# Broadcasting the mean and rstd of a layer norm through a DRAM scratch, in an eight-core encoder block on Trainium2

## The chip, the cores and the metric

The kernel runs on all 8 cores of one Trainium2 chip, with the same program on each core and no exchange between cores. The metric is the device time in microseconds (us) of the slowest core. Inside a core the engines are PE (TensorE, matrix products), DVE (VectorE), ACT (ScalarE), POOL (GpSimd) and SP (SyncE, which here only issues DMAs). Each engine runs its own list of instructions in order and waits on semaphores.

## The reference

One encoder block works on `x` of 4 sequences, 4096 tokens, 1024 channels. What matters here is the convolution branch and what is merged with it:

```
a = a_val * sigmoid(a_gate)                     # two products with w_in
a = depthwise_conv(a, w_dw, width 31) + b_dw
mu   = mean over the 1024 channels of a         # per token
rstd = rsqrt(mean((a - mu)^2) + 1e-5)           # per token
y_conv = silu((a - mu) * rstd * ln_g + ln_b) @ w_conv_out
merged = gateA * y_conv + gateB * y_pool        # y_pool: pooling branch
h = h + merged @ w_o
h = h + swiglu(rms_norm(h));  out = rms_norm(h)
```

The mean and the rstd are one number per token, and each is applied to all 1024 channels of that token.

## The kernel before, in words

Each core has 2048 tokens and works on them in two tiles of 1024 tokens; a tile has two blocks `b` of 512 tokens. Channels lie on partitions (8 groups `c` of 128) and tokens in the free dimension. A tile goes through these stages:

1. P1 (`P1_STEPS`): products with `w_in`, convolution and pooling. `conv(c)` (line 511) leaves the convolution output in `d_sb[:, c, b, :]`, and DVE adds it and its square up over `c` into `acc_s[:, b, :]` and `acc_q[:, b, :]` (128 x 512, f32).
2. P2 (`P2_STEPS`, a list written by hand): G steps (`gates`, line 656, four groups of 8 matmuls of 512 columns, each evicted by a Tanh on ACT), P steps (`pool_out`, line 673, two groups, evicted by DVE into `sgB`) and Y steps (`conv_out`, line 685, one group for one block `b`, which reads `actT[:, 0..7, b, :]`, evicted by two DVE instructions). The order is G0 G1 P0 P1 G2 P2 G3 Y0.0 Y1.0 Y2.0 Y0.1 Y1.1 Y2.1, and then the rest.
3. The product with `w_o`, the SwiGLU with its two large products (`ffn`, `down`), and the stores.

The layer norm is laid into P2 by the table `ln_plan` (line 646), whose keys are (G step, group in it). After the first two groups of G0, `ln_sums(b)` (line 598) sums `acc_s` and `acc_q` over the partitions with 8 matmuls against a column of ones, each with one output column, so that the sums of token 128*j + p stand on partition p, column j. Four small DVE instructions and one power on POOL (line 611) make mean and rstd of the block: 4 columns each in `lnst`, on 128 partitions.

To be applied, the two must stand on every partition, with the 512 tokens in the free dimension. Before, this takes two functions for each block `b` and each of mean and rstd (`w` = 0 and 1). `ln_spread(b, w)` (line 613) writes `tn` = identity times the column, 128 x 512 in f32, on DVE (line 619). `ln_bcast(b, w)` (line 621) multiplies it in f32 with the 128 x 128 matrix of ones on PE, which puts the values on all partitions of a PSUM bank, and ACT copies the bank into `acc_s` or `acc_q` (line 626), whose sums are no longer needed. The trace shows each such f32 product as two matmul records. The `order` rows show it as one row.

`ln_chunk(c, b)` (line 631) then applies mean and rstd to one channel group of one block: two DVE instructions (lines 637, 638) and a Silu on ACT (line 639) into `actT`. There are 16 chunks in a tile. They stand in the queue `lnq`, and `ln_step` takes one of them after each group of 8 matmuls in the G, P and Y steps.

PSUM has 8 banks that `nb()` gives out in turn, one to a group of matmuls, so PE can be at most 8 groups ahead of the evictions. Weights come in units of 256 KB by DMAs that POOL issues (`prefetch`, line 352) into a ring of 21 buffers. SP issues the other loads: in the first tile, ahead of P2, `invc` and two loads of `gb` (lines 888 to 890), and after step Y2.1 three loads of `xt` (`xres_load`, line 697), which lie over `acc_s`, `acc_q` and `sq` in memory. `xbar_transpose` (line 427) issues DMA transposes from SP in later stages.

Of the kernel before, what the change touches and what calls it, by code (L numbers as in the profile page):

```python
# [12 lines left out]
KC = 8  # L13
# [202 lines left out]
def build_nc():  # L216
    nc = bass.Bass("TRN2", target_bir_lowering=False)
    S = Sched(nc)
# [97 lines left out]
    def nb():  # L316
        b = bank[0]
        bank[0] = (b + 1) % 8
        return b

    def sem(name):
        return nc.alloc_semaphore(name)
# [5 lines left out]
    SP = Rec("sp", sem("s_sp"))  # L328
    gb_sem = [Prod(sem(f"d_gb{i}"), 16) for i in range(3)]
    tr_sem = [Prod(sem(f"d_tr{i}"), 16) for i in range(17)]  # L330
    wpt_sem = [Prod(sem(f"d_wpt{i}"), 16) for i in range(2)]
    cst = [Prod(sem(f"d_cst{i}"), 16) for i in range(3)]
    ring_sem = [Prod(sem(f"d_wr{i}"), 16) for i in range(RING)]
# [264 lines left out]
    def ln_sums(b):  # L598
        bk = nb()
        for w, acc in ((0, acc_s), (1, acc_q)):  # L600
            for j in range(4):
                o = psum[bk][:, w * 4 + j:w * 4 + j + 1]
                mm(o, acc[:, b, j * 128:j * 128 + 128], ones[:, 0:1], True, True, w == 1 and j == 3)
        mean4, msq4, rstd4 = (lnst[:, b * 16 + 4 * k:b * 16 + 4 * k + 4] for k in range(3))
        ps4, pq4 = psum[bk][:, 0:4], psum[bk][:, 4:8]
        S.op(DVE, lambda e: e.tensor_scalar(out=mean4, in0=ps4, scalar1=1.0 / D, scalar2=None, op0=ALU.mult), [ps4], [mean4])
        S.op(DVE, lambda e: e.tensor_tensor(out=msq4, in0=mean4, in1=mean4, op=ALU.mult), [mean4], [msq4])
        S.op(DVE, lambda e: e.scalar_tensor_tensor(out=msq4, in0=pq4, scalar=1.0 / D, in1=msq4, op0=ALU.mult, op1=ALU.subtract),
             [pq4, msq4], [msq4])
        S.op(DVE, lambda e: e.tensor_scalar(out=msq4, in0=msq4, scalar1=LN_EPS, scalar2=None, op0=ALU.add), [msq4], [msq4])  # L610
        S.op(POOL, lambda e: e.tensor_tensor(out=rstd4, in0=msq4, in1=nhalf[:, 0:4], op=ALU.pow), [msq4, nhalf[:]], [rstd4])

    def ln_spread(b, w):
        src = lnst[:, b * 16 + 8 * w:b * 16 + 8 * w + 4]
        dg = tn[w * 2 + b][:]
        o3 = dg.rearrange("p (j t) -> p j t", j=4)
        i0 = ident[:].unsqueeze(1).to_broadcast([128, 4, 128])
        i1 = src.unsqueeze(2).to_broadcast([128, 4, 128])
        S.op(DVE, lambda e: e.tensor_tensor(out=o3, in0=i0, in1=i1, op=ALU.mult), [ident[:], src], [dg])

    def ln_bcast(b, w):
        bm = nb()
        dg = tn[w * 2 + b][:]
        mm(psum[bm][:], ones[:], dg, True, True, True)
        dst, pmi = (acc_s, acc_q)[w][:, b, :], psum[bm][:]
        S.op(ACT, lambda e: e.activation(out=dst, in_=pmi, func=AF.Copy), [pmi], [dst])

    ti = [0]
    lnq = []
# [11 lines left out]
    def ln_step():  # L641
# [2 lines left out]
            ln_chunk(c, b)  # L644

    ln_plan = {
        (0, 0): (lambda: ln_sums(0),),
        (0, 1): (lambda: ln_sums(1),),
        (0, 2): (lambda: ln_spread(0, 0), lambda: ln_spread(0, 1)),
        (0, 3): (lambda: ln_bcast(0, 0), lambda: ln_spread(1, 0), lambda: ln_spread(1, 1)),  # L650
        (1, 0): (lambda: ln_bcast(0, 1), lambda: lnq.extend((k, 0) for k in range(KC))),
        (1, 1): (lambda: ln_bcast(1, 0),),
        (1, 2): (lambda: ln_bcast(1, 1), lambda: lnq.extend((k, 1) for k in range(KC))),
    }

    def gates(c):
# [411 lines left out]
```

How the kernel before makes its waits and increments, by code:

```python
def replay(e, rec):  # L205
    for o in rec.ops:
        if o[0] == "wait":
            e.wait_ge(o[1], o[2])
        elif o[0] == "ins":
            r = o[1](e)
            if o[2]:
                r.then_inc(rec.sem, 1)
        else:
            e.dma_start(out=o[1], in_=o[2]).then_inc(o[3], 16)
# [212 lines left out]
    def xbar_transpose(rec, dsem, out_ap, in_ap):  # L427
        rg, wg = S._sets([in_ap], [out_ap], (), ())
        S._waits(rec, S._deps(rg, wg, dsem, dsem.count + 16))
        dsem.count += 16
        rec.ops.append(("ins", lambda e: e.dma_start_transpose(out_ap, in_ap).then_inc(dsem.sem, 16), False))
```

## Time and profile before

| what | value |
|---|---|
| three timed runs | 1027.54, 1030.3 and 1162.77 us; median 1030.3 |
| the profiled execution, its own time | 1026.95 us |
| its span on the slowest core (core 7) | 1025.4 us |
| spans of the eight cores | 1020.5 to 1025.4 us |
| granted TensorE clock, mean over the span, core 7 | 0.991 |
| PE busy, of the span | 98% |
| DVE / ACT / POOL busy, of the span | 42% / 27% / 17% |

The profiled execution is one run of the program. Its span goes from the first to the last instruction of core 7. Its own time is 1.55 us longer (1026.95 - 1025.4), which lies around the span. "Busy" of an engine counts its work and not its waits. The first tile's P2 begins at 155.3 us, the second tile's at 641.6 us.

### The profile page before, as it was taken

The page shows a single profiled execution, that of the slowest core. Times are in us where ns is not written, and L with a number is a line of the kernel's source. Part 1 is how long each engine was busy: PE and PEld are TensorE (multiplying, and loading weights), DVE is VectorE, ACT ScalarE, POOL GpSimd, SP SyncE. Part 2 cuts the span into 40 slices and gives each one's busy share as a digit, 9 for nine tenths or more (in the row PEclk, how much of TensorE's full clock was granted, in tenths as well). Part 3 has the DMA queues.
Part 4 walks back from the last instruction along what each step waited for, and adds up shares of the span by engine and source line. Part 5 has one row for each costly group of instructions (what it writes and reads, how often), then busy time and mean ns, then how long its engine had stood idle before and what let it go on. Part 6 is the DMA issues. An engine that isn't in the chain of part 4 may idle for free.

```text
span 1025.4 us, 16277 instructions; the slowest of 8 cores (1020.5 to 1025.4 us)
## 1 busy us (share of the span) xinstructions
PE 1001.4 (98%) x5606; PEld 475.1 (46%) x5606; DVE 431.4 (42%) x654; ACT 281.7 (27%) x490; POOL 178.3 (17%) x328
## 2 busy tenths in 40 slices
PE   6899999999999999999999999999999999999996
PEld 3556555444444444444444444544444444444442
DVE  5466555742472323211345566574247212111133
ACT  4234455512132222211113334451213211111111
POOL 3211422011122211110231111101113111111010
PEclk8999999999999999999999999999999999999999
DMA  8698997343389877640939988334336954554022
GB/s 223 98 203 180 182 246 131 86 81 62 64 190 175 162 112 126 94 66 1 175 104 250 205 147 163 59 92 73 62 67 152 152 75 73 78 81 65 1 72 102
DMA packets 80481, 121.29 MB, mean 118 GB/s; under 512 B 30833, under 2 KB 30833, under 8 KB 80402
## 3 DMA queue, kind: packets, MB, share of 16 engines
q0 software_dynamic: 38592, 70.27, 43.3%
q1 hardware_dynamic: 39506, 41.86, 16.4%
q10 hardware_dynamic: 2304, 8.13, 2.0%
q8 instruction: 47, 0.77, 0.3%
q14 instruction: 32, 0.26, 0.1%
HBM read 159.59 MB, written 8.39 MB: 164 GB/s over the span
## 4 chain that ended last, share of the span: by engine, by line
PE 96%; DMA 2%; DVE 1%; ACT 1%; issue 0%; SPq 0%; DVEq 0%; POOLq 0%; ACTq 0%
PE ps L382 90%; PE ps L522 6%; DMA h<-xe 2%; PE ps L414 0%; ACT sqj L392 0%; DVE ub L404 0%; SPq L214 0%; DVEq L949 0%; DVE s L559 0%; ACT sqj L750 0%; DVE h L748 0%; DVE uT L423 0%; POOLq L949 0%; ACT psb L545 0%; ACT sg L486 0%
## 5 line engine op out<-in xcount | busy, mean ns | idle before, releaser
L382 PE MATMUL ps<-vT,wr 128*128 128x512 bf16 x1408 | 304.9, 379 | 0.0
L382 PE MATMUL ps<-uT,wr 128*128 128x512 bf16 (+1 forms) x1472 | 290.5, 356 | 2.1 <-ACT sqj L392 2.1
L214 POOL DMA_DIRECT2D wr<-wst x268 | 142.9, 535 | 688.9 <-PE ps L382 631.2
L382 PEld LDWEIGHTS ps<-vT,wr 128*128 128x128 bf16 x1408 | 137.6, 98 | 165.2
L382 PEld LDWEIGHTS ps<-uT,wr 128*128 128x128 bf16 x1472 | 143.8, 99 | 143.8 <-issue 12.3
L730 DVE TENSOR_TENSOR fT<-ps,sgf 128x512 bf16<-128x512 f32 x88 | 60.9, 692 | 217.5 <-PE ps L382 195.4
L382 PE MATMUL ps<-wr,fT 128*128 128x512 bf16 x704 | 152.3, 379 | 0.0
L729 ACT ACTIVATE sgf<-ps 128x512 f32<-128x512 f32 x88 | 52.5, 597 | 229.0 <-PE ps L382 229.0
L382 PEld LDWEIGHTS ps<-wr,fT 128*128 128x128 bf16 x704 | 68.9, 98 | 83.1
L522 PE MATMUL ps<-rep,wr 128*32 128x512 bf16 x1024 | 59.9, 388 | 2.1 <-DVE s L559 2.1
L748 DVE TENSOR_TENSOR h<-ps,h 128x512 f32<-128x512 f32 x32 | 22.1, 692 | 84.3 <-PE ps L382 84.3
L382 PE MATMUL ps<-m2T,wpf 128*128 128x512 bf16 x256 | 57.5, 379 | 0.0
L382 PE MATMUL ps<-actT,wr 128*128 128x512 bf16 x256 | 57.2, 379 | 0.0
L750 ACT ACTIVATE sqj<-h 128x512 bf16<-128x512 f32 x32 | 20.1, 630 | 134.0 <-DVE h L748 134.0
L382 PE MATMUL ps<-wr,mergedT 128*128 128x512 bf16 x256 | 55.6, 379 | 0.0
L679 DVE SCALAR_TENSOR_TENSOR sgB<-sgB,ps 128x512 f32<-128x512 f32 x32 | 21.9, 686 | 72.7 <-PE ps L382 72.5
L665 ACT ACTIVATE sgA<-ps,pc_s 128x512 f32<-128x512 f32 x32 | 21.8, 681 | 102.5 <-PE ps L382 101.5
L392 ACT ACTIVATE sqj<-h 128x1024 bf16<-128x1024 f32 x24 | 25.4, 1057 | 64.1 <-DVE h L708 53.4
L522 PEld LDWEIGHTS ps<-rep,wr 128*32 128x32 bf16 x1024 | 26.7, 98 | 33.1 <-issue 9.7
L486 ACT ACTIVATE sg<-ps 128x352 f32<-128x352 f32 (+1 forms) x40 | 20.7, 517 | 69.4 <-PE ps L382 57.8
L382 PEld LDWEIGHTS ps<-m2T,wpf 128*128 128x128 bf16 x256 | 25.0, 98 | 30.2
L382 PEld LDWEIGHTS ps<-wr,mergedT 128*128 128x128 bf16 x256 | 25.0, 98 | 30.2
(75 smaller groups left out, 616.0 us busy)
## 6 DMA issues: line engine op xcount, KB each, us to landing
wr<-wst POOLq DMA_DIRECT2D x268, 256.0 KB, 5.4
rep<-aT SPq DMA_DIRECT2D x256, 65.8 KB, 5.5
xt<-xe SPq DMA_DIRECT2D x24, 512.0 KB, 4.5
out<-h ACTq DMA_DIRECT2D x15, 512.0 KB, 2.8
h<-xe SPq DMA_DIRECT2D x8, 512.0 KB, 7.2
wpt<-wpt SPq DMA_DIRECT2D x4, 256.0 KB, 9.3
gb_s<-gb SPq DMA_DIRECT2D x2, 512.0 KB, 10.9
out<-h ACTq DMA_DIRECT2D x1, 256.0 KB, 2.1
```

Of the source, the lines that this page charges most:

```text
L214: e.dma_start(out=o[1], in_=o[2]).then_inc(o[3], 16)
L382: S.op(PE, lambda e: e.matmul(out, lhsT=lhsT, rhs=rhs, start=start, stop=stop), [lhsT, rhs], [out], signal=signal)
L392: S.op(ACT, lambda e: e.activation(out=sqj[0:n, :], in_=src, func=AF.Square, scale=1.0 / 32.0, accum_out=ms), [src], [sqj[0:n, :], ms])
L486: S.op(ACT, lambda e: e.activation(out=sgo, in_=pgi, func=AF.Tanh, scale=0.5), [pgi], [sgo])
L522: S.op(PE, lambda e, o=o, lt=lt, r_=r_, q=q, j=j: e.matmul(o, lhsT=lt, rhs=r_, start=(q == 0), stop=(q == 7), tile_position=(0, 32 * j)), ...
L665: S.op(ACT, lambda e, o=o, p_=p_, bia=bia: e.activation(out=o, in_=p_, func=AF.Tanh, bias=bia, scale=0.5), [p_, bia], [o])
L679: S.op(DVE, lambda e, t=t, p_=p_: e.scalar_tensor_tensor(out=t, in0=t, scalar=1.0, in1=p_, op0=ALU.add, op1=ALU.mult), [p_, t], [t])
L729: S.op(ACT, lambda e: e.activation(out=so, in_=pgi, func=AF.Silu), [pgi], [so])
L730: S.op(DVE, lambda e: e.tensor_tensor(out=fo, in0=pui, in1=so, op=ALU.mult), [pui, so], [fo])
L748: S.op(DVE, lambda e, ho=ho, pdi=pdi: e.tensor_tensor(out=ho, in0=pdi, in1=ho, op=ALU.add), [pdi, ho], [ho])
L750: S.op(ACT, lambda e, ho=ho, sh=sh: e.activation(out=sqj[:, 0:512], in_=ho, func=AF.Square, scale=1.0 / 32.0, accum_out=sh), [ho], [sqj[:, ...
```

## The change

`ln_spread` is gone, and `ln_bcast(b)` now does mean and rstd of a block by DMAs from SP: one DMA stores the 8 columns of `lnst` (128 partitions x 8 values of 4 bytes) into a DRAM scratch `lscr[b]`, in the order of the tokens, so that the values of neighbouring partitions stand 4 bytes apart and those of one partition 512 bytes apart. SP waits on the semaphore of this store (`ls_sem`). Then two DMAs read the 512 mean values and the 512 rstd values for every one of the 128 partitions and write them into `acc_s[:, b, :]` and `acc_q[:, b, :]` (256 KB each). Both count on one semaphore (`lb_sem[b]`), and a reader waits for both. In `lnst` the rstd takes the columns beside the mean.

In `ln_plan`, `ln_bcast(b)` follows `ln_sums(b)` in the first two groups of G0. The chunks of block 0 are queued one group later than before, at (1, 1); those of block 1 at (1, 2) as before.

```diff
--- before.py
+++ after.py
@@ -226,6 +226,8 @@
     ic_d = nc.dram_tensor("invc", [128, 32], F32, kind="ExternalInput")
     out_d = nc.dram_tensor("out", [TOK, D], F32, kind="ExternalOutput")
 
+    lscr = nc.dram_tensor("lscr", [2, 2, 512], F32, kind="Internal")
+
     base0 = (nc.sbuf_base + 63) // 64 * 64
     top = nc.sbuf_top
 
@@ -328,6 +330,8 @@
     SP = Rec("sp", sem("s_sp"))
     gb_sem = [Prod(sem(f"d_gb{i}"), 16) for i in range(3)]
     tr_sem = [Prod(sem(f"d_tr{i}"), 16) for i in range(17)]
+    ls_sem = [Prod(sem(f"d_ls{i}"), 16) for i in range(2)]
+    lb_sem = [Prod(sem(f"d_lb{i}"), 16) for i in range(2)]
     wpt_sem = [Prod(sem(f"d_wpt{i}"), 16) for i in range(2)]
     cst = [Prod(sem(f"d_cst{i}"), 16) for i in range(3)]
     ring_sem = [Prod(sem(f"d_wr{i}"), 16) for i in range(RING)]
@@ -601,7 +605,7 @@
             for j in range(4):
                 o = psum[bk][:, w * 4 + j:w * 4 + j + 1]
                 mm(o, acc[:, b, j * 128:j * 128 + 128], ones[:, 0:1], True, True, w == 1 and j == 3)
-        mean4, msq4, rstd4 = (lnst[:, b * 16 + 4 * k:b * 16 + 4 * k + 4] for k in range(3))
+        mean4, msq4, rstd4 = (lnst[:, b * 16 + 4 * k:b * 16 + 4 * k + 4] for k in (0, 2, 1))
         ps4, pq4 = psum[bk][:, 0:4], psum[bk][:, 4:8]
         S.op(DVE, lambda e: e.tensor_scalar(out=mean4, in0=ps4, scalar1=1.0 / D, scalar2=None, op0=ALU.mult), [ps4], [mean4])
         S.op(DVE, lambda e: e.tensor_tensor(out=msq4, in0=mean4, in1=mean4, op=ALU.mult), [mean4], [msq4])
@@ -610,20 +614,19 @@
         S.op(DVE, lambda e: e.tensor_scalar(out=msq4, in0=msq4, scalar1=LN_EPS, scalar2=None, op0=ALU.add), [msq4], [msq4])
         S.op(POOL, lambda e: e.tensor_tensor(out=rstd4, in0=msq4, in1=nhalf[:, 0:4], op=ALU.pow), [msq4, nhalf[:]], [rstd4])
 
-    def ln_spread(b, w):
-        src = lnst[:, b * 16 + 8 * w:b * 16 + 8 * w + 4]
-        dg = tn[w * 2 + b][:]
-        o3 = dg.rearrange("p (j t) -> p j t", j=4)
-        i0 = ident[:].unsqueeze(1).to_broadcast([128, 4, 128])
-        i1 = src.unsqueeze(2).to_broadcast([128, 4, 128])
-        S.op(DVE, lambda e: e.tensor_tensor(out=o3, in0=i0, in1=i1, op=ALU.mult), [ident[:], src], [dg])
-
-    def ln_bcast(b, w):
-        bm = nb()
-        dg = tn[w * 2 + b][:]
-        mm(psum[bm][:], ones[:], dg, True, True, True)
-        dst, pmi = (acc_s, acc_q)[w][:, b, :], psum[bm][:]
-        S.op(ACT, lambda e: e.activation(out=dst, in_=pmi, func=AF.Copy), [pmi], [dst])
+    def ln_bcast(b):
+        S.wait_prod(SP, lb_sem[b])
+        o_ = lscr.ap()[b].rearrange("w (j p) -> p (w j)", p=128)
+        i_ = lnst[:, b * 16:b * 16 + 8]
+        rg, wg = S._sets([i_], [], (), ())
+        S._waits(SP, S._deps(rg, wg, ls_sem[b], ls_sem[b].count + 16))
+        ls_sem[b].count += 16
+        SP.ops.append(("ins", lambda e: e.dma_start(out=o_, in_=i_, allow_slow_non_contiguous=True).then_inc(ls_sem[b].sem, 16), False))
+        S.wait_prod(SP, ls_sem[b])
+        tot = lb_sem[b].count + 32
+        for w in range(2):
+            src = bass.AP(tensor=lscr, offset=(b * 2 + w) * 512, ap=[[0, 128], [1, 512]])
+            S.dma(SP, lb_sem[b], (acc_s, acc_q)[w][:, b, :], src, val=tot)
 
     ti = [0]
     lnq = []
@@ -644,13 +647,10 @@
             ln_chunk(c, b)
 
     ln_plan = {
-        (0, 0): (lambda: ln_sums(0),),
-        (0, 1): (lambda: ln_sums(1),),
-        (0, 2): (lambda: ln_spread(0, 0), lambda: ln_spread(0, 1)),
-        (0, 3): (lambda: ln_bcast(0, 0), lambda: ln_spread(1, 0), lambda: ln_spread(1, 1)),
-        (1, 0): (lambda: ln_bcast(0, 1), lambda: lnq.extend((k, 0) for k in range(KC))),
-        (1, 1): (lambda: ln_bcast(1, 0),),
-        (1, 2): (lambda: ln_bcast(1, 1), lambda: lnq.extend((k, 1) for k in range(KC))),
+        (0, 0): (lambda: ln_sums(0), lambda: ln_bcast(0)),
+        (0, 1): (lambda: ln_sums(1), lambda: ln_bcast(1)),
+        (1, 1): (lambda: lnq.extend((k, 0) for k in range(KC)),),
+        (1, 2): (lambda: lnq.extend((k, 1) for k in range(KC)),),
     }
 
     def gates(c):
```

PE, first tile, from the sums of block 1 to the first P step (`wr` are the ring's weights, `tn` the identity products, `m2T` the input of the P steps); before:

```order
L382 MATMUL ps<-ones_s,acc_q 128x1 x4
L382 MATMUL ps<-uT,wr_62 128x512 x8
L382 MATMUL ps<-uT,wr_63 128x512 x8
L382 MATMUL ps<-tn_139,ones_s 128x512
L382 MATMUL ps<-uT,wr_43 128x512 x8
L382 MATMUL ps<-tn_141,ones_s 128x512
L382 MATMUL ps<-uT,wr_44 128x512 x8
L382 MATMUL ps<-tn_140,ones_s 128x512
L382 MATMUL ps<-uT,wr_43 128x512 x8
L382 MATMUL ps<-tn_142,ones_s 128x512
L382 MATMUL ps<-uT,wr_44 128x512 x8
L382 MATMUL ps<-m2T,wpf 128x512 x32
```

and now:

```order
L386 MATMUL ps<-ones_s,acc_q 128x1 x4
L386 MATMUL ps<-uT,wr_62 128x512 x8
L386 MATMUL ps<-uT,wr_63 128x512 x8
L386 MATMUL ps<-uT,wr_43 128x512 x8
L386 MATMUL ps<-uT,wr_44 128x512 x8
L386 MATMUL ps<-uT,wr_43 128x512 x8
L386 MATMUL ps<-uT,wr_44 128x512 x8
L386 MATMUL ps<-m2T,wpf 128x512 x32
```

The four products of `tn` with `ones_s` between the groups of 8 are gone from PE; nothing else on it has another place.

SP, first tile, from the last convolution input to the first `xt` load, with the waits; before:

```order
L214 DMA invc_s<-invc 128x32
L214 DMA gb_s<-gb 128x1024 x2
L214 DMA xt_90<-xe 128x1024 [waits s_act,s_dve]
L214 DMA xt_91<-xe 128x1024 [waits s_act,s_dve]
L214 DMA xt_92<-xe 128x1024
```

and now:

```order
L214 DMA invc_s<-invc 128x32
L214 DMA gb_s<-gb 128x1024 x2
L624 DMA lscr<-lnst 128x8x1 [waits s_pool]
L214 DMA acc_s<-lscr 128x512 [waits d_ls0,s_dve,s_pe]
L214 DMA acc_q<-lscr 128x512 [waits s_dve]
L624 DMA lscr<-lnst 128x8x1 [waits s_pool]
L214 DMA acc_s<-lscr 128x512 [waits d_ls1,s_dve,s_pe]
L214 DMA acc_q<-lscr 128x512 [waits s_dve]
L214 DMA xt_90<-xe 128x1024 [waits d_lb0,s_dve,d_lb1]
L214 DMA xt_91<-xe 128x1024 [waits s_dve]
```

Six DMAs stand between the `gb` loads and the `xt` loads. The store of block 0 waits for POOL's power. The first broadcast waits for that store, and the store of block 1 stands behind both broadcasts of block 0.

DVE, first tile, from the second of the four identity products (`tn` from `ident_s`) to the first eviction of a P step (`sgB`); L637 and L638 are a chunk; before:

```order
L619 TENSOR_TENSOR tn_141<-ident_s,lnst 128x512
L619 TENSOR_TENSOR tn_140<-ident_s,lnst 128x512
L619 TENSOR_TENSOR tn_142<-ident_s,lnst 128x512
L637 TENSOR_TENSOR tn_139<-d_sb,acc_s 128x512
L638 TENSOR_TENSOR tn_139<-tn_139,acc_q 128x512
L637 TENSOR_TENSOR tn_140<-d_sb,acc_s 128x512
L638 TENSOR_TENSOR tn_140<-tn_140,acc_q 128x512
L637 TENSOR_TENSOR tn_141<-d_sb,acc_s 128x512
L638 TENSOR_TENSOR tn_141<-tn_141,acc_q 128x512
L637 TENSOR_TENSOR tn_142<-d_sb,acc_s 128x512
L638 TENSOR_TENSOR tn_142<-tn_142,acc_q 128x512
L679 SCALAR_TENSOR_TENSOR sgB_131<-sgB_131,ps 128x512
```

and now, from the last small instruction of the sums of block 1 (L640 and L641 are a chunk):

```order
L614 TENSOR_SCALAR lnst<-lnst 128x4
L640 TENSOR_TENSOR tn_139<-d_sb,acc_s 128x512
L641 TENSOR_TENSOR tn_139<-tn_139,acc_q 128x512
L640 TENSOR_TENSOR tn_140<-d_sb,acc_s 128x512
L641 TENSOR_TENSOR tn_140<-tn_140,acc_q 128x512
L640 TENSOR_TENSOR tn_141<-d_sb,acc_s 128x512
L641 TENSOR_TENSOR tn_141<-tn_141,acc_q 128x512
L679 SCALAR_TENSOR_TENSOR sgB_131<-sgB_131,ps 128x512
```

The identity products (three of the first tile's four stand above) are gone, and three chunks instead of four stand ahead of the first `sgB` eviction, because the chunks are queued one group later. 

## Rows read from the trace of the kernel before

**Rows 1.** The page: busy time, TensorE clock by slice, chain that ended last

```profile
PE 1001.4 (98%) x5606; PEld 475.1 (46%) x5606; DVE 431.4 (42%) x654; ACT 281.7 (27%) x490; POOL 178.3 (17%) x328
...
PEclk8999999999999999999999999999999999999999
...
PE 96%; DMA 2%; DVE 1%; ACT 1%; issue 0%; SPq 0%; DVEq 0%; POOLq 0%; ACTq 0%
```

**Rows 2.** Groups of instructions by line, whole span

```profile
L382 PE MATMUL ps<-tn,ones_s 128*128 128x512 f32 x16 | 8.2, 592 | 0.0
...
L619 DVE TENSOR_TENSOR tn<-ident_s,lnst 128x512 f32<-128x512 bf16 x8 | 5.2, 688 | 0.7 <-POOL lnst L611 0.7
```

**Rows 3.** PE in order of time, first tile: start us, us, instruction

```profile
155.32 1.91 PE L382 MATMUL ps<-uT,wr 128*128 128x512 bf16 x8
...
165.67 1.02 PE L382 MATMUL ps<-tn,ones_s 128*128 128x512 f32 x2
166.53 1.90 PE L382 MATMUL ps<-uT,wr 128*128 128x512 bf16 x8
168.26 1.02 PE L382 MATMUL ps<-tn,ones_s 128*128 128x512 f32 x2
...
200.26 4.05 PE L382 MATMUL ps<-actT,wr 128*128 128x512 bf16 x18
```

**Rows 4.** All engines in order of time, first tile, POOL's power and first chunk

```profile
160.14 1.04 POOL L611 TENSOR_TENSOR lnst<-lnst,nhalf_s 128x4 f32<-128x4 f32 x1 [3.65 <-DVE lnst L610]
...
167.62 0.69 DVE L637 TENSOR_TENSOR tn<-d_sb,acc_s 128x512 f32<-128x512 f32 x1 [1.05 <-ACT acc_s L626]
```

**Rows 5.** The same view, DVE and ACT in the middle of the chunks

```profile
184.03 0.68 DVE L679 SCALAR_TENSOR_TENSOR sgB<-sgB,ps 128x512 f32<-128x512 f32 x1
...
184.63 0.68 DVE L637 TENSOR_TENSOR tn<-d_sb,acc_s 128x512 f32<-128x512 f32 x1
...
186.02 0.69 DVE L637 TENSOR_TENSOR tn<-d_sb,acc_s 128x512 f32<-128x512 f32 x1
...
198.97 0.81 ACT L639 ACTIVATE actT<-tn,pc_s 128x512 bf16<-128x512 f32 x1
```

**Rows 6.** POOL's power and PE in the second tile, in order of time

```profile
641.59 1.91 PE L382 MATMUL ps<-uT,wr 128*128 128x512 bf16 x8
...
646.40 1.04 POOL L611 TENSOR_TENSOR lnst<-lnst,nhalf_s 128x4 f32<-128x4 f32 x1 [3.67 <-DVE lnst L610]
```

**Rows 7.** Line 431, the DMA transposes: issue to landing

```profile
DMA to landing us min/median/max: 3.1/3.7/8.7
```

**Rows 8.** DMA queues, 325 to 336 us, one transpose and one xt load

```profile
q1 hardware_dynamic: 1199, 0.79, 46.4%
...
uT<-ub SPq DMA_TRANSPOSE x1, 8.7
```

**Rows 9.** SP's DMA issues in order of time, first tile, before P2

```profile
142.19 0.90 SPq L214 DMA_DIRECT2D gb_s<-gb  x2
```

**Rows 10.** The page: DMA queues and issues, us to landing at the end

```profile
q0 software_dynamic: 38592, 70.27, 43.3%
...
xt<-xe SPq DMA_DIRECT2D x24, 512.0 KB, 4.5
...
gb_s<-gb SPq DMA_DIRECT2D x2, 512.0 KB, 10.9
out<-h ACTq DMA_DIRECT2D x1, 256.0 KB, 2.1
```

**Rows 11.** Five-microsecond stretches: PEclk, DMA share and GB/s stand last

```profile
160.00:165.00 5.00, 5.00 (x33) 3.26 (x31) 1.95 (x6) 1.37 (x2) 2.28 (x2) 1.00 1.09 187
165.00:170.00 5.00, 5.00 (x21) 2.25 (x20) 1.98 (x3) 2.57 (x4) 1.26 (x3) 1.00 0.96 161
170.00:175.00 5.00, 5.00 (x21) 2.27 (x20) 3.50 (x6) 3.31 (x6) 0.53 (x1) 1.00 0.06 10
645.00:650.00 5.00, 5.00 (x34) 3.31 (x34) 1.63 (x9) 0.69 (x1) 1.21 (x2) 1.00 0.01 2
```

## The prediction

> **What bounds the kernel now.** I read the page first. PE is busy for 98% of the span, the chain that ended last runs over PE for 96% of it, and the granted clock is 0.9 or more in all slices but the first [rows 1]. In the stretches that matter here it is 1.00, the 2.4 GHz level [rows 11]. So whatever leaves PE's list shortens the kernel by its own length, as long as nobody makes PE wait afterwards. Next I looked for what the change removes. The list of groups has 16 matmul records of `ps<-tn,ones_s`, two for each f32 product: 8 products, four to a tile [rows 2]. Their price is not the 8.2 us of that row, because neighbouring matmuls overlap. It has to be read from PE in order of time: such a product begins at 165.67 and the next group of 8 at 166.53, so it takes 0.86 us of PE's time. The group of 8 takes 168.26 - 166.53 = 1.73 us [rows 3]. Last I looked for the slack behind the mean and rstd, on DVE and ACT, since the change makes them come later.
>
> **The change part by part.**
>
> *Removed from PE:* 8 products by 0.86 us = 6.9 us, all on the path. *Removed from DVE:* 8 identity products of 0.69 us, and from ACT as many copies; both engines are busy for 42% and 27% of the span [rows 1, 2], and at this place they stand ahead of the chunks, so I count them at nothing in themselves. They did set when the chunks began.
>
> *Added on SP's queue:* per block one store and two broadcasts. SP is idle there: behind the six DMAs of a tile wait only the three `xt` loads, which need the last chunk anyway. Issuing two such loads took SP 0.90 us [rows 9], and nobody waits for that.
>
> *Added wait:* the first chunk on DVE now waits until mean and rstd of block 0 have landed. Call this time T, and S the time from the store's issue to its landing. The store can go when POOL's power ends, 160.14 + 1.04 = 161.2 us [rows 4], so at about 161.3. Then the two broadcasts (512 KB together) follow, with a landing time like a 512 KB load, 4.5 us, against 10.9 us for the two `gb` loads beside full queues [rows 10]; with SP's wake-up I take 5. T = 161.3 + S + 5. Before, the first chunk began at 167.6 [rows 4].
>
> *How late may T be?* Behind the waiting chunk on DVE stand all 16 chunks and the `sgB` evictions of the P steps; behind the Silu on ACT stand the Tanh evictions of the G steps. PE goes on until it needs a bank or a chunk's result. A chunk takes DVE 186.02 - 184.63 = 1.39 us, an eviction between two chunks 0.60 (184.03 to 184.63), the Silu 0.81 [rows 5]. Six evictions (P0, P1, P2) fall among the 16 chunks: 16 x 1.39 + 6 x 0.60 = 25.8, with the Silu and a handover of 0.1 the last `actT` is there at T + 26.8. The reader is Y0.1. Y0.0 began at 200.26 [rows 3]; without four products of 0.86 it begins at 196.8, Y0.1 three groups later at 202.0, and its eighth matmul, which reads the last channel group, 7/8 of a group later at 203.5. So T may be as late as 203.5 - 26.8 = 176.7. The eight banks give a looser bound: by the same walk over ACT's list, T up to some 179.
>
> *S* is not in this trace: no transfer has 4-byte pieces. The store has 128 x 8 = 1024 of them, since neither side joins two values (the values of a partition lie 512 bytes apart in DRAM); over 16 engines that is 64 each. The nearest thing in number is a DMA transpose: in 325 to 336 us the queue q1 moved 1199 packets and 0.79 MB; one `xt` load of 0.52 MB is 128 of them, so a transpose is about 1070 packets of 256 bytes. They cost 0.464 x 16 x 11 / 1199 = 68 ns each, and the transpose landed after 8.7 us, beside weight loads [rows 8]; the median of all transposes is 3.7 and the least 3.1 [rows 7]. The dear end is the mean packet of the weight queue q0, 0.433 x 16 x 1025.4 / 38592 = 184 ns [rows 10]. In the first tile the DMA engines are full from 160 to 170 us (share 1.09 and 0.96) and idle from 170 to 175 (0.06); in the second they are idle at the store (0.01) [rows 11]. So S is bounded from below by 3.1. From above, 64 packets of 184 ns plus 2.1 us, the shortest landing of a store to DRAM [rows 10], give 13.9 with idle queues; with the queues full each packet also waits for one of q0, if they take turns: 64 x (184 + 68) ns + 2.1 = 18.2. I take the transposes, which agree in number of packets and differ in size: S = 8.7 in the first tile, 3.7 in the second.
>
> *First tile:* T = 161.3 + 8.7 + 5 = 175.0, which is 1.7 before the limit: no stall. The second block's store goes at about 171 and its broadcasts land at about 171 + 3.7 + 5 + 2 = 182, while DVE asks for them after 8 chunks and 4 evictions, at T + 13.5 = 188.5. *Second tile:* P2 begins at 641.59 against 155.32 [rows 3, 6], so the limit is 176.7 + 486.3 = 663.0; the power ends at 647.4 [rows 6], T = 647.6 + 3.7 + 5 = 656.3. No stall, 6.7 us to spare.
>
> By the Trainium skill ("DMA: Bandwidth & Descriptors", Rules for kernel authors) a pattern whose last dimension is not contiguous becomes one descriptor per element; that would be the same 1024, and no run here shows it yet.
>
> *Sum, against the profiled execution's own time:* 1026.95 - 6.9 + 0 = 1020.05. The values 1026.95, 1027.54 and the median 1030.3 of before have a mean of 1028.3, 1.3 above the profiled one, so I forecast 1020.05 + 1.35 = 1021.4 us.
>
> **The rivals.** *A, the late store, slower than before.* If 4-byte writes to DRAM cost much more than 256-byte packets to SBUF, T passes the limit and PE waits for it microsecond by microsecond. First tile: T - 176.7 = S - 10.4; for its second block, T2 = 161.3 + S + 0.9 (two issues) + S + 5 against T + 13.5, so S - 12.6 more; the second tile gives about the same. With one S for all, 4S - 46 us. That eats the gain of 6.9 at S = 13.2, which is the point from which the kernel is slower than before; it costs 2% beyond that (27.5 us in all) at S = 18.4. At my upper bounds (S = 18.2, then 13.9) the stalls are 7.8 + 5.6 + 3.5 + 1.3 = 18.2, and the time is 1021.4 + 18.2 = 1039.6. For it: the slack in the first tile is only 1.7 us by my sum, the queues are full there, neighbouring values of 4 bytes are written by different descriptors, and DVE has no room to catch up (1.39 + 0.60 in a P group against 1.73 of PE). Against it: 68 ns a packet gives 4.4 us of work, and the DMA engines fall idle at 170 us. The Trainium skill ("DMA: Bandwidth & Descriptors", Specifications) says that pieces under 512 bytes make the DMA engine read, modify and write. If that doubles a packet of 68 ns, S grows by 4.4 to 13.1 in the first tile and 8.1 in the second, and the stalls are 2.7 + 0.5 = 3.2: the time would be 1024.6. The 256-byte packets of the transposes are under that size too and landed in 3.7 us, but in SBUF, so the trace neither confirms nor denies it.
>
> *B, part of the gain lost.* S between 10.4 and 13.2 in the first tile, or broadcasts near the 10.9 us of the `gb` loads: T at 177 to 182, a stall of 1 to 5 us, once or twice. Time about 1025.
>
> *C, the freed time is handed back elsewhere.* The broadcasts write 2 MB more into SBUF beside the weight loads, and PE takes the weights 3.5 us sooner in each P2. If the weights were near their limit, PE would meet that as a new wait on `wr`, and the time would stay at about 1028. Against it: the idle DMA stretch from 170 us on, and no `PE <- DMA` anywhere on a 96% PE chain.
>
> **How the numbers follow.** Forecast 0.55, A 0.20, B 0.13, C 0.07; the remaining 0.05 is what I haven't seen, in either direction. The likeliest gives 1021.4. Its own range is 1017 to 1025: 3 to 4 us for the spread of the runs. Up to 1034 the range takes in B, C and the milder part of A (S to about 15), so that about 2 in 10 is left out, nearly all above. A difference of 2% is about what a measurement of this kernel tells from no change. Nothing here can give 20 us, so faster by over 2% gets 0.03. Slower by over 2% needs S over 18 or a second effect: 0.10, half of A. The rest, 0.87, is within 2%.
>
> **What would show it.** Right: no `tn,ones_s` records; the groups of 8 in G1 start 1.73 us apart; the first chunk starts between 172 and 177 us; Y0.0 at about 196.8; PE has no idle time between 155 and 260. For S, the landing time of `lscr<-lnst`: 3 to 10 us. A is right if that is over 13 us and PE waits for `actT` or for a bank at Y0.1 and before. B shows as one such wait of a few us in the first tile only. C shows as PE waiting for `wr`. The prediction is wrong as to its mechanism if PE waits in P2 while the chunks come in time, or if the kernel gains more than 9 us.

## The result and the profile after

The changed kernel takes 1070.2 us in the median of 4 runs (1067.14 to 1072.51), against 1027.54 for the kernel before (1025.57 to 1030.3, 3 runs); the ratio is 1.041, with an interval of 1.037 to 1.046. It is slower by 4%, where 1021.4 us were forecast and 1034 was the upper end of the range. Runs in which a whole die was disturbed are left out, which below leaves one run of e4 and of e11 and two of e10. The profile is of core 3, the slowest; the cores' spans go from 1058.2 to 1071.0 us.

The page, with the rows that answer to [rows 1], and the waits of PE (us in total, times, longest):

```profile
PE 1004.1 (94%) x5590; PEld 473.2 (44%) x5590; DVE 424.3 (40%) x646; ACT 277.7 (26%) x482; POOL 177.5 (17%) x328
...
PEclk9999999799999999999999999978999999999999
...
PE ps L386 76%; DMA lscr<-lnst 7%; PE ps L526 5%; SPq L214 2%; DMA acc_q<-lscr 2%; DMA h<-xe 2%; DMA rep<-aT 1%; DVE tn L640 1%; PE ps L418 0%; DVE sgB L679 0%; ACT sgA L665 0%; DVE ub L408 0%; ACT sqj L396 0%; DVE tn L641 0%; ACT actT L642 0%
```

```profile
PE ps L386 <- ACT sgA L665: 38.3, 4, 17.6
PE ps L386 <- ACT actT L642: 6.2, 6, 1.1
```

The products are gone, but PE's busy share has fallen from 98% to 94%. DMA holds 11% of the chain that ended last, most of it the store `lscr<-lnst`. PE waits 38.3 us for a Tanh eviction and 6.2 us for chunks. The clock has a 7 in two slices, one in each P2.

PE in order of time, the two P2, which answers to [rows 3]:

```profile
156.18 1.89 PE L386 MATMUL ps<-uT,wr 128*128 128x512 bf16 x8
...
159.61 10.56 PE L386 MATMUL ps<-uT,wr 128*128 128x512 bf16 x48
...
176.91 3.63 PE L386 MATMUL ps<-uT,wr 128*128 128x512 bf16 x16
197.39 6.03 PE L386 MATMUL ps<-uT,wr 128*128 128x512 bf16 x16 [16.85 <-ACT sgA L665]
203.26 3.62 PE L386 MATMUL ps<-m2T,wpf 128*128 128x512 bf16 x16
...
215.22 6.59 PE L386 MATMUL ps<-actT,wr 128*128 128x512 bf16 x29 [1.41 <-ACT sgA L665]
222.83 0.38 PE L386 MATMUL ps<-actT,wr 128*128 128x512 bf16 x1 [1.02 <-ACT actT L642]
224.23 0.38 PE L386 MATMUL ps<-actT,wr 128*128 128x512 bf16 x1 [1.02 <-ACT actT L642]
225.68 5.52 PE L386 MATMUL ps<-actT,wr 128*128 128x512 bf16 x17 [1.07 <-ACT actT L642]
231.04 1.24 PE L386 MATMUL ps<-m2T,wpf 128*128 128x512 bf16 x5
```

```profile
686.18 3.63 PE L386 MATMUL ps<-uT,wr 128*128 128x512 bf16 x16
707.37 5.34 PE L386 MATMUL ps<-uT,wr 128*128 128x512 bf16 x16 [17.55 <-ACT sgA L665]
```

The six groups of G0 and G1 now run without a gap (48 matmuls in 10.4 us, 1.73 us a group), so the 0.86 us of each product is really gone. Then PE stands still for 16.85 us in the first tile and 17.55 in the second, both times before the third group of G2, which needs the bank of a Tanh that stands on ACT behind the first chunk's Silu. In the stop the granted clock has fallen to 0.50, the 1.2 GHz level: the 16 matmuls from 197.39 take 5.87 us until 203.26, where 3.46 are usual, and the 17 from 225.68 take 5.36 instead of 3.7.

```profile
190.00:195.00 5.00, 0.00 (x0) 0.00 (x0) 0.69 (x1) 0.00 (x0) 0.00 (x0) 0.50 0.09 7
```

(Busy time by engine, then PEclk, DMA share and GB/s.) SP's issues in order of time show where the time goes (start us, us):

```profile
158.67 0.38 SPq L624 DMA_DIRECT2D lscr<-lnst  x1
186.70 0.33 SPq L214 DMA_DIRECT2D acc_s<-lscr  x1
...
187.59 0.38 SPq L624 DMA_DIRECT2D lscr<-lnst  x1
197.61 0.32 SPq L214 DMA_DIRECT2D acc_s<-lscr  x1
```

```profile
668.00 0.39 SPq L624 DMA_DIRECT2D lscr<-lnst  x1
677.74 0.33 SPq L214 DMA_DIRECT2D acc_s<-lscr  x1
...
678.81 4.79 SPq L624 DMA_DIRECT2D lscr<-lnst  x1
714.88 0.32 SPq L214 DMA_DIRECT2D acc_s<-lscr  x1
```

SP issues a broadcast when it has seen the store land, so the distance is S, SP's wake-up included: 28.0 and 10.0 us for the two blocks of the first tile, 9.7 and 36.1 in the second. Over the eight cores S is 14.4 to 29.1 and 10.0 to 21.3 in the first tile, 9.4 to 19.3 and 20.5 to 36.1 in the second. The prediction took 8.7 and 3.7. The broadcasts are late too (the view of DMA issues, us to landing; the row of its own is DVE's wait for them):

```profile
acc_s<-lscr SPq DMA_DIRECT2D x4, 256.0 KB, 9.7
acc_q<-lscr SPq DMA_DIRECT2D x4, 256.0 KB, 10.5
...
lscr<-lnst SPq DMA_DIRECT2D x4, 4.0 KB, 18.9
```

```profile
DVE tn L640 <- DMA acc_q<-lscr: 76.0, 4, 34.1
```

What happens between is seen in the DMA queues of 162 to 166 us, of 166 to 170 and of 170 to 174 (packets, MB, share of the 16 engines):

```profile
q0 software_dynamic: 220, 0.39, 65.7%
q1 hardware_dynamic: 990, 0.00, 19.5%
...
wr<-wst POOLq DMA_DIRECT2D x2, 256.0 KB, 19.9
```

```profile
DMA packets 7, 0.01 MB, mean 2 GB/s; under 512 B 3, under 2 KB 3, under 8 KB 7
...
q0 software_dynamic: 4, 0.01, 8.4%
```

```profile
q0 software_dynamic: 84, 0.17, 112.1%
```

Nearly all 1024 pieces pass through the DMA engines in the first four microseconds (990 packets, 19.5% of 16 engines, so 0.195 x 16 x 4 / 990 = 12.6 ns each; in the second tile 1040 packets at 11.7% from 668 to 672 us, 7.2 ns each). SP sees their landing at 186.7, 20 us after nearly all of them had passed. For 4 us almost nothing else moves, 7 packets. Then the weights move again, but slowly: the 84 packets from 170 to 174 us take 1.121 x 16 x 4 / 84 = 0.85 us each, and 17 packets at 42.7% from 174 to 178 take 1.6 us each, where the mean before was 184 ns. From 182 to 186 us it is 0.18 us again. The two weight units issued between 162 and 166 us take 19.9 us to land, against a median of 5.8 on the page. So the cost is not in the engines' work on small packets, and it holds up the other queue. That it lies behind the engines, where the writes are finished, is inferred: no record shows the memory.

The 36.1 us of the last store have a second part. It is issued at 678.81, behind the broadcasts of block 0, which took 18.9 and 26.0 us to land, and its pieces pass only after 696 us (1023 packets until 700, some 60 of them the broadcast's by their size, and 101 more until 706):

```profile
q1 hardware_dynamic: 1023, 0.13, 40.4%
```

From 706 to 712 us the core moves one packet in all, and the store has landed at 714.9.

The sum by these rows, slowest core after against slowest core before: waits at the chunks 38.3 + 6.2 = 44.5, lower clock after the stops some 2.4 + 1.7 + 1.7 + 1.7 = 7.5 (the last taken equal to its twin of the first tile), removed products -6.9, together 45 us, against spans of 1071.0 - 1025.4 = 45.6.

### The profile page after: what moved, and what is told of

It is laid out like the page before. It is cut to its first block, busy times and chain, and to the rows that moved or that the text cites. A ratio compares the mean times of both kernels' runs of the same rounds, so it can differ in the third digit from the quotient of the medians.

```text
span 1071.0 us, 16234 instructions; the slowest of 8 cores (1058.2 to 1071.0 us)
## 1 busy us (share of the span) xinstructions
PE 1004.1 (94%) x5590; PEld 473.2 (44%) x5590; DVE 424.3 (40%) x646; ACT 277.7 (26%) x482; POOL 177.5 (17%) x328
## 4 chain that ended last, share of the span: by engine, by line
PE 82%; DMA 11%; SPq 2%; DVE 2%; issue 1%; ACT 1%; DVEq 0%; POOL 0%; POOLq 0%; ACTq 0%
PE ps L386 76%; DMA lscr<-lnst 7%; PE ps L526 5%; SPq L214 2%; DMA acc_q<-lscr 2%; DMA h<-xe 2%; DMA rep<-aT 1%; DVE tn L640 1%; PE ps L418 0%; DVE sgB L679 0%; ACT sgA L665 0%; DVE ub L408 0%; ACT sqj L396 0%; DVE tn L641 0%; ACT actT L642 0%
## 5 line engine op out<-in xcount | busy, mean ns | idle before, releaser
L386 PE MATMUL ps<-actT,wr 128*128 128x512 bf16 x256 | 63.0, 400 | 10.1 <-ACT actT L642 6.2
L750 ACT ACTIVATE sqj<-h 128x512 bf16<-128x512 f32 x32 | 20.2, 631 | 133.7 <-DVE h L748 133.7
L640 DVE TENSOR_TENSOR tn<-d_sb,acc_s 128x512 f32<-128x512 f32 x32 | 21.9, 686 | 76.0 <-DMA acc_q<-lscr 76.0
L642 ACT ACTIVATE actT<-tn,pc_s 128x512 bf16<-128x512 f32 x32 | 26.1, 814 | 80.8 <-DVE tn L641 80.3
L386 PEld LDWEIGHTS ps<-actT,wr 128*128 128x128 bf16 x256 | 25.8, 102 | 45.6 <-issue 19.9
## 6 DMA issues: line engine op xcount, KB each, us to landing
gb_s<-gb SPq DMA_DIRECT2D x2, 512.0 KB, 10.4
```

Of the source, the lines that this page charges most:

```text
L386: S.op(PE, lambda e: e.matmul(out, lhsT=lhsT, rhs=rhs, start=start, stop=stop), [lhsT, rhs], [out], signal=signal)
L640: S.op(DVE, lambda e: e.tensor_tensor(out=t, in0=dso, in1=mean, op=ALU.subtract), [dso, mean], [t])
L642: S.op(ACT, lambda e: e.activation(out=ao, in_=t, func=AF.Silu, bias=lb, scale=lg), [t, lg, lb], [ao])
L750: S.op(ACT, lambda e, ho=ho, sh=sh: e.activation(out=sqj[:, 0:512], in_=ho, func=AF.Square, scale=1.0 / 32.0, accum_out=sh), [ho], [sqj[:, ...
```

## The experiments

The question was what makes the landing late. Eleven kernels were run, on three chips (e1 to e4, e5 to e8, e9 to e11), each against the kernel before on its own chip (medians 1028.1 to 1028.7 us). The edits are shortened to the lines that matter; e3 to e11 all have the line with `gb_d` that is shown with e3. Where the broadcasts read `gb` in place of the scratch (runs e3 to e11), mean and rstd are not applied, but every instruction has its size.

### Fewer pieces, and none

**e1.** Runs of 16 bytes: the sums are taken over every fourth token, so that a partition holds four neighbours.

```diff
-mm(o, acc[:, b, j * 128:j * 128 + 128], ones[:, 0:1], ...)
+mm(o, acc[:, b, :].rearrange("p (t j) -> p t j", j=4)[:, :, j], ones[:, 0:1], ...)
-o_ = lscr.ap()[b].rearrange("w (j p) -> p (w j)", p=128)
+o_ = lscr.ap()[b].rearrange("w (p j) -> p w j", j=4)
-i_ = lnst[:, b * 16:b * 16 + 8]
+i_ = lnst[:, b * 16:b * 16 + 8].rearrange("p (w j) -> p w j", j=4)
```

> The sums are taken over every fourth token, so that a partition holds four neighbouring tokens and the store is 256 runs of 16 bytes instead of 1024 of 4; all else is as in the changed kernel. Theory N (each small write to DRAM costs, one after another, at the memory): the wait for the store, 10 to 28 us in the changed kernel, falls to about a quarter plus a fixed part of 2 us, so 4 to 9 us, PE's waits at the chunks shrink from 44 us to under 5, and the time is about 1023 to 1030 us. Theory B (the bytes or the DRAM address are slow, not the number of pieces): the store still lands after 10 to 28 us and the time stays near 1070.

Measured: 1033.0 us, ratio 1.006 (1.004 to 1.008). S is 6.7 to 11.1 us in the first tile and 2.2 to 8.0 in the second, and PE has no wait for `sgA` or `actT` on the slowest core. So the store's wait fell as theory N has it. The time did not come down to the 1023 to 1030 expected, for reasons of the run's own. The first is weights of 128 columns that stand 16 bytes apart.

```profile
L386 PEld LDWEIGHTS ps<-ones_s,acc_s x32: 308/329/337, 155.3 to 654.3; 128*128 128x128 f32 x32
```

```profile
155.49 1.81 PE L386 MATMUL ps<-ones_s,acc_s 128*128 128x1 f32 x8
...
159.03 3.58 PE L386 MATMUL ps<-uT,wr 128*128 128x512 bf16 x8
162.40 1.82 PE L386 MATMUL ps<-ones_s,acc_s 128*128 128x1 f32 x8
```

A load takes 329 ns where it took 191 with neighbouring columns, and the sums of a block 3.54 us (155.49 to 159.03) where they took 1.72, four times in the kernel: 7.3 us. The second is the clock, which the sum of the experiment did not have: it fell during the first of these sums and was granted at 0.50 from 159 to 170 us of the first tile, while PE was busy without a gap, so that the group between the sums took 3.37 us (159.03 to 162.40) instead of 1.73; in the second tile the same group took 3.10 and the clock was back by 661 us. What set it off is not shown.

**e2.** Rows of 512 bytes: PE turns the eight columns round first.

```diff
+def ln_turn(b):
+    idf = tn[3][:, 0:128]                      # f32 identity, copied from ident in each tile
+    po, ro = psum[bk][0:8, 0:128], tn[2][0:8, b * 128:b * 128 + 128]
+    mm(po, lnst[:, b * 16:b * 16 + 8], idf, True, True, True)
+    S.op(DVE, lambda e: e.tensor_copy(out=ro, in_=po), [po], [ro])
-o_ = lscr.ap()[b].rearrange("w (j p) -> p (w j)", p=128);  i_ = lnst[:, b * 16:b * 16 + 8]
+o_ = lscr.ap()[b].rearrange("w (j p) -> (w j) p", p=128);  i_ = tn[2][0:8, b * 128:b * 128 + 128]
-    (0, 0): (ln_sums(0), ln_bcast(0)),  (0, 1): (ln_sums(1), ln_bcast(1)),
+    (0, 0): (ln_sums(0),),  (0, 1): (ln_sums(1),),
+    (0, 2): (ln_turn(0), ln_bcast(0)),  (0, 3): (ln_turn(1), ln_bcast(1)),
```

> Mean and rstd are turned on PE first (a product of the 8 columns with an f32 identity, copied from PSUM by DVE), and the store is 8 rows of 512 bytes. Adds 2 small f32 products and 3 small DVE copies to a tile. Theory N: the store lands after 2 to 3 us, PE does not wait in the chunks, and the kernel gains the 6.9 us of the removed products less some 0.3 us for each of 4 turns: 1022 to 1024 us, ratio to before 0.994 to 0.996. Theory R (a hot spot: 128 rows of each broadcast read the same 2 KB on every core at once): the broadcasts still land after 10 to 25 us, PE waits 10 us or more, and the time is above before's.

Measured: 1024.0 us in the median of 5 runs, ratio 0.9966 (0.9951 to 0.998): of the kernels that apply mean and rstd the only one that is faster than before, by 0.3%. PE in order of time:

```profile
165.21 0.38 PE L386 MATMUL ps<-tn,lnst 128*8 128x128 f32 x2
165.53 1.91 PE L386 MATMUL ps<-uT,wr 128*128 128x512 bf16 x8
...
198.85 10.52 PE L386 MATMUL ps<-actT,wr 128*128 128x512 bf16 x47
```

```profile
649.75 0.31 SPq L633 DMA_DIRECT2D lscr<-tn  x1
651.11 0.36 SPq L214 DMA_DIRECT2D acc_s<-lscr  x1
```

A turn costs PE 0.32 us (165.21 to 165.53). The first block's store of 8 rows lands after 1.4 us in the second tile (649.75 to 651.11) and 4.3 to 6.5 in the first; the second block's, behind the broadcasts, after 4.5 to 6.4 and 3.9 to 7.1. PE has no wait for a bank behind the chunks on any core, and none for a chunk but 2.0 us on core 7. The time is at the upper end of what was expected. Theory R is out: the broadcasts, 128 reads of one 2 KB row, land after 4.5 and 5.4 us (medians of the slowest core).

**e4.** No store; SP waits for POOL and issues the broadcasts, which read `gb`.

> No store at all; SP waits for POOL's power and then issues the two broadcasts of each block, which read the gains from another tensor, so mean and rstd are not applied. If the store is the whole cost (theories N, L, B): the broadcasts land after 4 to 6 us, PE does not wait in the chunks, and the time is the forecast 1021 to 1023 us. Theory R (reads of one 2 KB row by 128 partitions are slow): the broadcasts land after 10 us or more and PE waits for the chunks.

Measured: 1021.44 us, one run, 6.7 below the kernel before on that chip. The rest of the prediction, 6.9 us off the path and broadcasts that are early enough, gives the forecast number once the store is away.

### The spacing

**e3, e6, e11.** The same 1024 values of 4 bytes in one DMA, 256, 64 and 32 bytes apart. **e5.** The same, 4 bytes apart, as in the changed kernel.

```diff
-lscr = nc.dram_tensor("lscr", [2, 2, 512], F32, kind="Internal")
+lscr = nc.dram_tensor("lscr", [2, 2, 512, 64], F32, kind="Internal")    # 16 in e6, 8 in e11
-o_ = lscr.ap()[b].rearrange("w (j p) -> p (w j)", p=128)
+o_ = lscr.ap()[b].rearrange("w (j p) s -> p (w j) s", p=128)[:, :, 0:1]
-src = bass.AP(tensor=lscr, offset=(b * 2 + w) * 512, ap=[[0, 128], [1, 512]])
+src = bass.AP(tensor=gb_d, offset=w * 512, ap=[[0, 128], [1, 512]])     # alone in e5
```

> The same 1024 writes of 4 bytes, but each in its own 256 bytes of DRAM, so that no two share a line; the broadcasts read the gains from another tensor in place of the scratch, so mean and rstd are not applied. Theory N (number of partial writes): the store lands as late as in the changed kernel, 10 to 28 us, and the time is about 1060 to 1070. Theory L (neighbouring 4-byte values collide in one line or one bank and go one after another): the store lands after 3 to 6 us and the time is 1022 to 1030.

> The changed kernel's own dense store (1024 values of 4 bytes, neighbours 4 bytes apart), waited for as there, but the broadcasts read the gains from another tensor, so mean and rstd are not applied. It differs from the spread run in the spacing alone and from the changed kernel in the source of the broadcasts alone. Theory L (neighbouring values collide): the stores land after 10 to 36 us and the time is 1060 to 1070. Theory S (it was the source: reading lines that were just written is what is slow): the stores land within 10 us in the second tile and the time is near the spread run's 1028.

> As the spread run, with the 4-byte values 64 bytes apart instead of 256. Theory L with lines of 64 bytes or less: as the spread run, first store of the second tile in 3 to 4 us, time 1026 to 1030. If the unit in which they collide is larger (256 bytes or more), or it is the small area of DRAM that counts: the stores land between the two, 5 to 20 us in the second tile, and the time is 1035 or more.

> As the runs with spaced values, with the values 32 bytes apart (two to 64 bytes). If values collide within 32 bytes only: as at 64 and 256 bytes apart, 3 to 4 us for the first store of the second tile and 1026 to 1030 us. If the unit is 64 bytes: two writes to a line instead of sixteen, so somewhat slower, 4 to 8 us, and 1028 to 1038 us. Theory area: between dense and spaced, since the area is 32 KB instead of 64.

| run | bytes between values | time, us | ratio to before | S, second tile, first block | S, first tile, first block |
|---|---|---|---|---|---|
| e5 | 4 | 1080.4 | 1.052 (1.045 to 1.059) | 11.3 to 18.0 | 13.7 to 37.0 |
| e11 | 32 | 1032.9 (one run) | | 3.2 to 6.9 | 9.3 to 20.4 |
| e6 | 64 | 1028.0 | 0.9996 (0.998 to 1.001) | 3.0 to 4.4 | 13.1 to 20.5 |
| e3 | 256 | 1027.8 | 0.9997 (0.9986 to 1.0007) | 2.7 to 3.8 | 13.5 to 18.9 |

Each S is the spread over the eight cores, read from SP's issues as above. The slowest core of the dense run e5 and of e6:

```profile
680.86 0.39 SPq L624 DMA_DIRECT2D lscr<-lnst  x1
698.83 0.33 SPq L214 DMA_DIRECT2D acc_s<-gb  x1
```

```profile
652.99 0.39 SPq L624 DMA_DIRECT2D lscr<-lnst  x1
656.87 0.33 SPq L214 DMA_DIRECT2D acc_s<-gb  x1
```

The number of pieces, their size, the DMA and the wait are the same; only the distance differs, and 11.3 to 18.0 us become 3.0 to 4.4. That speaks against theory N, which wanted e3 as slow as the changed kernel, and against theory S. Theory L stands. Its time for e5, 1060 to 1070, was too low; why e5 is some 10 us above the changed kernel is open. e11 lies close to the spaced runs; from its single time nothing finer can be read than that most of the harm is gone at 32 bytes. What e3 and e6 still lack to e4's 1021.4 is the first tile: there S is 13 to 20 us in both, and PE waits 5.1 us (e3) and 7.6 us (e6) for `sgA`, on the slowest core. The queues of e6 from 170 to 174 us show why:

```profile
q0 software_dynamic: 289, 0.52, 100.3%
q1 hardware_dynamic: 292, 0.00, 7.6%
```

The pieces take turns with the weight packets one for one, and the weights fill the engines.

e1 belongs to this as well: its runs of 16 bytes stand four to 64 bytes, and they landed after 2.7 to 5.1 us (second tile, first block). So what is dear is 64 bytes that 16 single writes share; shared by four of 16 bytes, or by two of 4 bytes (e11), they were not.

**e9, e10.** A shared line, or a small area? 16 neighbours still share 64 bytes; in e9 each such line has its own 1024 bytes, in e10 the lines are dense. Both store by 8 DMAs of 16 partitions.

```diff
+for g in range(8):
+    o_ = lscr.ap()[b].rearrange("w (j g) s -> g s w j", g=8)[g, 0:16]    # lscr [2, 2, 32, 256] in e9, [2, 2, 32, 16] in e10
+    i_ = lnst[16 * g:16 * g + 16, b * 16:b * 16 + 8].rearrange("p (w j) -> p w j", j=4)
```

> Which is it, values that share 64 bytes, or a small area of DRAM? Here 16 neighbouring values still share 64 bytes, but each such line has its own 1024 bytes, so the area is 16 times as large as in the dense store (64 KB for a block, as in the run with values 64 bytes apart). The store is split into 8 DMAs of 16 partitions; SP waits for all of them; the broadcasts read the gains from another tensor, so mean and rstd are not applied. Theory line (values in one 64-byte line go one after another): stores land after 10 to 30 us, time 1050 to 1080. Theory area (a few banks take all the writes): as the runs with spaced values, 3 to 6 us in the second tile plus up to 3 us for the seven extra issues, time 1025 to 1035.

> The control of the run above: the same 8 DMAs of 16 partitions, with the lines one behind the other, which is the layout of the changed kernel. Under both theories the stores land after 10 to 30 us and the time is 1050 to 1085. If it is fast, splitting the DMA is itself a cure and the run above says nothing on the line.

Measured: e9 1086.0 us, ratio 1.056 (1.043 to 1.068); e10 1084.1 (mean of 1082.0 and 1086.2), ratio 1.054 (1.049 to 1.059). First stores land after 19.8 to 48.4 us in e9 and 31.1 to 40.9 in e10 (first tile), 10.4 to 26.8 and 12.9 to 24.7 (second). An area 16 times as large brings nothing if the lines stay shared; e6, with an area of the same size and no shared lines, is fast. So it is the values that share 64 bytes, and not the area. The split is no cure; that it does no harm of its own is read from e10 beside e5 (ratios 1.054 and 1.052), and a split store with 64 bytes for each value was not run. e9 is above the 1080 expected.

**e8.** The same 1024 pieces, written into SBUF.

```diff
-o_ = lscr.ap()[b].rearrange("w (j p) -> p (w j)", p=128)
+o_ = sq[b][:, 0:16].rearrange("p (c two) -> p c two", two=2)[:, :, 0:1]
```

> The same 1024 pieces of 4 bytes, waited for in the same way, but written into SBUF (every second element of 16 in each partition) instead of DRAM; the broadcasts read the gains from another tensor, so mean and rstd are not applied. If the price is of DRAM: the store lands after 3 to 4 us in the second tile and 5 to 18 us in the first (its 64 pieces an engine still take turns with weight packets), time 1021 to 1028. If 4-byte pieces are slow wherever they go: it lands after 10 us or more in the second tile too, time 1040 or more.

Measured: 1024.7 us, ratio 0.9968 (0.9954 to 0.9983). S is 2.5 to 5.0 us for the first block of the second tile, and 12.5 to 17.2 in the first tile. The first number is that of e6 (3.0 to 4.4): writes to DRAM that share nothing cost no more than writes to SBUF. That the collision is a matter of DRAM alone is not shown, since in SBUF no two partitions write into the same 64 bytes, only the 8 values of one stand together. The second number has nothing to do with DRAM: pieces to SBUF are just as late in the first tile, where the weights fill the queues.

### Does only the wait cost?

**e7.** The dense store as in e5, but SP does not wait for it (`S.wait_prod(SP, ls_sem[b])` taken out).

> The dense store is issued, but nothing waits for it; the broadcasts follow at once and read the gains from another tensor, so mean and rstd are not applied. Theory W (only the wait for the landing costs): the broadcasts land after 4 to 8 us, and the time is that of the run without a store, 1021 to 1023. Theory B (the backlog of small writes holds up every other transfer of the core, as the weight units that landed after 15 to 30 us suggest): the broadcasts land after 10 to 25 us, PE waits for the chunks, and the time is 1030 to 1055.

Measured: 1070.9 us, ratio 1.043 (1.034 to 1.051), above the 1055 at which theory B ended. The run to hold it against is e5, the same with the wait, at 1080.4 (1.045 to 1.059): without SP's wait some four fifths of the 52 us are still there, and the intervals overlap. Theory W is out. Four cores of the profiled run, and the waits of PE on core 4:

```profile
core 0: 1017.8 us, clock 0.996
core 1: 1066.1 us, clock 0.977
...
core 4: 1062.0 us, clock 0.977
core 5: 1029.6 us, clock 0.990
```

```profile
PE ps L386 <- ACT sgA L664: 27.5, 2, 23.4
PE ps L526 <- DMA rep<-aT: 10.2, 2, 8.4
```

The broadcasts land after 27.2 and 21.4 us (medians of core 1). In part they may only stand behind the store, for SP issues them on the same queue right after it. That does not hold for the loads of the other queue, nor for what moves before a core's own store. Core 4 stands 8.4 us before its last convolution of the second tile, at 667.7, for loads of `rep`; its own store of that tile is issued only at 679.8, and its first-tile stores were done long before. And on core 1 the weights crawl from 164 to 168 us, 0.728 x 16 x 4 / 36 = 1.3 us a packet, while no piece of its own store has passed yet (the first after 172):

```profile
q0 software_dynamic: 36, 0.06, 72.8%
```

Both point to the work of another core. Which one is inferred from pairs and not shown: in 0 and 1, 2 and 3, 4 and 5, 6 and 7 one span is 32 to 48 us over the other (2 and 3: 1022.8 and 1056.3; 6 and 7: 1021.1 and 1056.1), and core 5's store goes at 654.6 on its own clock. In e5's profiled run three of the pairs differ by 21 to 31 us, and the longer core of each (0, 2, 7) waits 7.6 to 10.5 us in all for `rep`, most of it before its own store of the second tile; in the kernel before such waits are 1.8 us at most. In the second run of e7 the pairs differ by only 2 to 19 us. Cores 0, 2 and 6 of e7 stay at 1017.8 to 1022.8 us, though their broadcasts land after 14.7 to 20.2 us (medians): issued at once, most of them are still within the slack of the prediction.

## Why the prediction was wrong

**Right:** the price of a product, 0.86 us, and that it is all on the path. So is the slack: P2 runs 2.6 us earlier on core 3 (its second group begins at 156.18, against 158.77 on the slowest core before), which puts the limit for T at 176.7 - 2.6 = 174.1. T was 194.3, the start of DVE's first chunk, 20.2 us later, and PE stood 16.85 + 1.41 + three waits for chunks of 1.02 to 1.07, together 21.4. The stop came at a bank first, as the looser bound allows: 179 - 2.6 = 176.4 for T by the prediction, 194.3 - 16.85 = 177.4 by the rows. e4 gave 1021.4 for the forecast without the store. Rival A had the right place and the right kind of cost, with a chance of 0.20 and at most 1039.6 us.

**The step that failed is S**, the term "I take the transposes, which agree in number of packets and differ in size". On core 3 the four stores took 28.0, 10.0, 9.7 and 36.1 us, where 8.7 stood for the first and 3.7 for the others; the first and the last are above even the upper bounds of 18.2 and 13.9. Two things were wrong in it, of different weight.

The large one: the bounds counted the work of the DMA engines per packet, 68 or 184 ns. The engines were done with 990 packets at 12.6 ns each, and the landing came 20 us later. That time goes away when each value has 64 bytes to itself (e6, e3) and stays when 16 share them, over whatever area (e5, e9, e10). No row of before showed such a write, and the transposes, whose pieces go to SBUF, could not bound it from above. The sentence in rival A that "neighbouring values of 4 bytes are written by different descriptors" named the right thing and gave it no price. e5 against e6 sets it: 52 us of 1028.

The small one: in the first tile single pieces take turns with the weight packets, as e6 shows. The bound with turns gave 18.2 us; e8 measured 12.5 to 17.2 and e6 13.1 to 20.5. The value taken, 8.7 from one transpose beside weight loads, was too low even without the collisions. With S = 13 to 20 for this one store the prediction's own S - 10.4 gives a stall of 3 to 10 us, which eats most or all of the gain of 6.9, and that is the result of e3 and e6 (1027.8 and 1028.0). In the changed kernel itself the turns are not what is seen: 990 pieces passed beside 220 weight packets.

**The added wait was treated as the only harm.** By the formula 4S - 46, core 3's values of S give 28.0 + 10.0 + 9.7 + 36.1 - 46 = 38 us, near the 44.5 that PE waited. But e7 shows that taking the wait away does not take the harm away: the weights and the `rep` loads are held up too, also on a core whose own store is not yet under way. The 5 us taken for the landing of the two broadcasts failed with it: block 0's took 18.9 and 26.0 us in the second tile. The lower clock after a stop, 7.5 us in all, was not in the sum.

**The rules named.** One descriptor per element ("DMA: Bandwidth & Descriptors" of the Trainium skill, Rules for kernel authors) agrees with the trace: the queue q1 has 5312 packets more than before, 4 stores of 1024 and 8 broadcasts of 128 are 5120. Read-modify-write under 512 bytes (the same page of the Trainium skill, Specifications) was priced by the prediction as a doubled packet, S = 8.1 us in the second tile. The runs do not support that price: with 64 bytes between them, as many small writes landed in 3.0 to 4.4 us there, like those to SBUF. Whether the engine reads before it writes is seen in no record.

**What stays open.** Whether the writes to one line go strictly one after another, or are repeated, is not seen in any record; nor whether the unit is 32 or 64 bytes, since e11 has one time and its two values to 64 bytes may be too few to cost. That it is the other core of the pair that holds a core up is inferred; the profiled runs of e7 and e5 point to it, the second run of e7 hardly.

## What to carry to other kernels

A scatter of single 4-byte values to DRAM, 16 of them to 64 bytes, is no small transfer: 4 KB of it took 10 to 36 us to land and held up other transfers meanwhile, waited for or not. Turn the data round first so that the store is whole rows (0.32 us on PE here), and the bounce through DRAM is cheap, 1.4 us for the store and about 5 for the broadcasts; that version beats both kernels, if the one before only by 0.3% (1024.0 us). Before a DMA that the trace has never shown is put on the path, bound its landing by what it writes and where, and not by packets of the same number that go elsewhere.

## What the runs showed of the hardware beyond this

- 1024 writes of 4 bytes to DRAM land in 3 to 4 us when 64 or 256 bytes apart (idle queues), and in 11 to 18 when 4 bytes apart; into SBUF in 2.5 to 5 (e3, e6, e5, e8; second tile, first block).
- The DMA engines pass such pieces at 7 to 13 ns each. The backlog shows afterwards: few packets or none for microseconds, or packets of the other queue at 0.85 to 1.6 us instead of 0.18 (a busy DMA row that moves few GB/s), beside transfers that don't land.
- A DMA of many small pieces is late beside a full weight queue, 12.5 to 20.5 us against 2.5 to 5, into DRAM or SBUF (e6, e8); 8 rows of 512 bytes were 4.3 to 6.5 against 1.4.
- Reading one 2 KB row 128 times, into 128 partitions, is a normal load: about 5 us for two of them (e2).
- An f32 weight load with columns 16 bytes apart takes 329 ns instead of 191 (e1).
